# Norm panels made row block by row block, with sums and row inside the next panel, and rows of scales made from a repeated column and the identity

## The reference, cut to what matters

```python
def rmsnorm(x, g):
    return x * lax.rsqrt(jnp.mean(x * x, axis=-1, keepdims=True) + EPS) * g

# first block, after its two mixers (y_ssd, y_attn)
mixed = (g_ssd * y_ssd + (attention @ w_attn_out) * g_attn) @ w_o
x = x + rmsnorm(mixed, post_mix_norm)
h = rmsnorm(x, pre_mlp_norm)
x = x + rmsnorm(jnp.square(jax.nn.relu(h @ w_mlp_in)) @ w_mlp_out, post_mlp_norm)
# second block
h = rmsnorm(x, norm_mix_g)            # then w_in: gates, mLSTM, latent attention
q_a  = rmsnorm(c_q, cq_norm_g) @ w_uq # c_q, c_kv, k_r are columns of h @ w_in
kv   = rmsnorm(c_kv, ckv_norm_g) @ w_ukv
# q_nope, q_rope, k_nope per head and k_rope get a norm each, then rotation, attention
x = x + concat(y_m, y_a) @ w_out
h = rmsnorm(x, norm_x_g)              # cross attention over 256 memory rows;
q = rmsnorm(h @ wq_x); k = rmsnorm(mem_n @ wkv_x part)   # per head
x = x + cross_attention @ wo_x
h = rmsnorm(x, norm_ffn_g)
x = x + jnp.square(jax.nn.relu(h @ w_ff1)) @ w_ff2
```

## Time and profile before

| | us |
|---|---|
| median of 3 timed runs | 2132.68 (2130.52 to 2133.43) |
| the profiled execution's own time | 2122.09 |
| its span, first to last instruction | 2120.0 |
| PE busy | 1972.2 (93%), mean granted clock 0.965 of 2.4 GHz |
| POOL busy | 1546.5 (73%) |
| DVE busy | 917.0 (43%) |
| ACT busy | 654.6 (31%) |
| time of the chain that ended last, by engine | PE 77%, POOL 11%, DVE 7% |

### The profile page before, as it was taken

One profiled execution on the slowest core, in us unless ns is written; L12 is line 12 of the kernel. 1 busy time (PEld: TensorE's weight loads), 2 busy tenths in 40 slices (PEclk: granted clock), 3 DMA queues, 4 the chain that ended last, 5 costly groups with the idle time before them and its releaser, 6 DMA issues.

```text
span 2120.0 us, 26435 instructions
## 1 busy us (share of the span) xinstructions
PE 1972.2 (93%) x9749; PEld 1625.7 (77%) x9749; DVE 917.0 (43%) x1732; ACT 654.6 (31%) x1216; POOL 1546.5 (73%) x1379
## 2 busy tenths in 40 slices
PE   6999999999999999799999989888697889999998
PEld 4888888887878888578888867756366767888887
DVE  4566666641034434354014226754654055401421
ACT  4466666542045651131011002342231142200200
POOL 7799988797845449779889887542709808988985
PEclk9999999999999999899999999997898899999999
DMA  7222222123332223213333321111102302333232
GB/s 214 81 60 60 60 60 72 49 63 103 83 112 62 67 70 123 93 43 99 99 99 99 100 82 50 49 41 60 40 1 80 116 4 79 99 99 95 89 98 75
DMA packets 212121, 165.97 MB, mean 78 GB/s; under 512 B 13438, under 2 KB 208321, under 8 KB 211634
## 3 DMA queue, kind: packets, MB, share of 16 engines
q1 hardware_dynamic: 207126, 147.61, 23.6%
q10 hardware_dynamic: 4892, 17.01, 2.4%
HBM read 161.43 MB, written 7.37 MB: 80 GB/s over the span
## 4 chain that ended last, share of the span: by engine, by line
PE 77%; POOL 11%; DVE 7%; issue 2%; ACT 2%; DMA 0%; DVEq 0%; SPq 0%; ACTq 0%; POOLq 0%
PE bank L393 58%; POOL w_lo L2548 5%; PE bank L413 4%; POOL w_hi L2543 3%; PE bank L1338 3%; PE bank L1314 2%; PE bank L1324 1%; PE bank L2104 1%; POOL x_features L651 1%; POOL arena L1031 1%; PE bank L2113 1%; PE bank L1013 1%; DVE arena L1786 1%; PE bank L991 1%; PE bank L459 1%
## 5 line engine op out<-in xcount | busy, mean ns | idle before, releaser
L2543 POOL TENSOR_TENSOR w_hi<-w_raw,one 128x512 fp32r<-128x512 f32 (+2 forms) x520 | 529.7, 1050 | 500.5 <-PE bank L393 436.6
L2548 POOL TENSOR_TENSOR w_lo<-w_raw,w_hi 128x512 fp32r<-128x512 f32 (+2 forms) x600 | 745.7, 1274 | 34.6 <-ACT w_hi L1176 30.2
L393 PE MATMUL bank<-h_hi,w_hi 128*128 128x512 f32 (+1 forms) x1144 | 459.1, 401 | 39.3 <-DVE h_lo L622 16.7
L393 PE MATMUL bank<-h_hi,w_lo 128*128 128x512 f32 (+1 forms) x1144 | 444.6, 389 | 0.0
L393 PE MATMUL bank<-h_lo,w_hi 128*128 128x512 f32 (+1 forms) x1144 | 444.4, 388 | 0.0
L393 PE MATMUL bank<-a_hi,w_hi 128*128 128x512 f32 x896 | 351.5, 392 | 12.7 <-POOL w_lo L2548 8.2
L393 PE MATMUL bank<-a_lo,w_hi 128*128 128x512 f32 x896 | 350.2, 391 | 0.0
L393 PE MATMUL bank<-a_hi,w_lo 128*128 128x512 f32 x896 | 350.1, 391 | 0.0
L393 PEld LDWEIGHTS bank<-h_hi,w_hi 128*128 128x128 f32 x1144 | 219.2, 192 | 95.8 <-issue 18.8
L393 PEld LDWEIGHTS bank<-h_hi,w_lo 128*128 128x128 f32 x1144 | 219.0, 191 | 44.5
L393 PEld LDWEIGHTS bank<-h_lo,w_hi 128*128 128x128 f32 x1144 | 219.7, 192 | 38.4 <-issue 0.2
(11 more groups left out here) (380 smaller groups left out, 2728.7 us busy)
## 6 DMA issues: line engine op xcount, KB each, us to landing
w_raw<-in_w_in SPq DMA_DIRECT2D x32, 1024.0 KB, 5.3
w_raw<-in_w_ff SPq DMA_DIRECT2D x32, 1024.0 KB, 5.5
w_raw<-in_w_mlp_in SPq DMA_DIRECT2D x16, 1024.0 KB, 5.3
w_raw<-in_w_mlp_out SPq DMA_DIRECT2D x16, 1024.0 KB, 5.8
w_raw<-in_w_in SPq DMA_DIRECT2D x25, 512.0 KB, 4.4
w_raw<-in_w_ssd_out SPq DMA_DIRECT2D x8, 1024.0 KB, 5.8
bias_rows<-bias_row ACTq DMA_DIRECT2D x1, 4096.0 KB, 15.8
w_raw<-in_w_attn_out SPq DMA_DIRECT2D x4, 1024.0 KB, 5.3
```

The lines of the kernel that those rows point to most:

```text
L393: mm = pe.matmul(bank[:, 0:ntok], a, b[:, koff + k, 0:ntok], start=(k == 0 and n == 0), stop=(k == L.kb - 1 and n == 2))
L2543: pool.tensor_tensor(w_hi[:, slot, part], raw[:, slot, part], one[:].broadcast_to([P, n]), ALU.mult).then_inc(split_hi, 1)
L2548: ins = pool.tensor_tensor(w_lo[:, slot, part], raw[:, slot, part], w_hi[:, slot, part].bitcast(F32), ALU.subtract)
```

## The change

`pe_panel_rows` is a panel in which both output blocks advance together: at each k it waits once and then makes six products. It serves the first panel of `L_attn_out`, `L_o`, both feed-forwards, `L_if` and `L_qx`. `pe_panel_with_root` is a panel with the sum behind its first block and the row behind the fourth k step of its second; it replaces sum and row around panel 1 of both feed-forwards and panel 0 of `L_m[0]`. The diagonals are gone: a row is made of one product per token tile, whose stationary operand is the column of scales repeated 128 times (stride 0) and whose moving operand is the identity. TensorE waits for the reciprocal in their place.

```diff
+        def pe_panel_rows(pe, L, i, X, ready, koff=0):
+            xh, xl = X
+            slot = (L.p0 + i) % 2
+            blocks = [(L.b0 + i * L.nb + j, off) for j, off in enumerate(L.offs)]
+            pe.wait_ge(split_ready, L.p0 + i + 1)
+            for blk, _ in blocks:
+                pe.wait_ge(acc_free, blk - 3)
+            for k in range(L.kb):
+                pe.wait_ge(*ready(k))
+                for blk, off in blocks:
+                    c = k * L.w + off
+                    wh, wl = w_hi[:, slot, c:c + P], w_lo[:, slot, c:c + P]
+                    for n, (a, b) in enumerate(((wh, xh), (wh, xl), (wl, xh))):
+                        mm = pe.matmul(banks[blk % 4][:], a, b[:, koff + k, :], start=(k == 0 and n == 0), stop=(k == L.kb - 1 and n == 2))
+                    if k == L.kb - 1:
+                        mm.then_inc(acc_ready, 1)
+
+        def pe_panel_with_root(pe, L, i):
+            pe_panel(pe, L, i, i, h_x, only=0)
+            root_sum_pe(pe)
+            pe_panel(pe, L, i, i, h_x, only=1, ks=range(0, 4))
+            root_row_pe(pe)
+            pe_panel(pe, L, i, i, h_x, only=1, ks=range(4, DB))
...
         def root_row_pe(pe):
-            pe.wait_ge(nx_diag, nx_n["sum"])
-            pe.matmul(NROW[:], ones[:], NROOT, start=True, stop=True).then_inc(nx_row, 1)
+            pe.wait_ge(nx_inverse, nx_n["sum"])
+            for t in range(T):
+                mm = pe.matmul(NROW[:, t * P:(t + 1) * P], nstat[:, t:t + 1].broadcast_to([P, P]), ident[:], start=True, stop=True)
+            mm.then_inc(nx_row, 1)
...
-            dve_link(dve.reciprocal(nstat, nstat))
+            dve.reciprocal(nstat, nstat).then_inc(nx_inverse, 1)
             row_dve(dve)
...
         def row_dve(dve):
-            n = nx_n["acc"] // DB
-            dve.tensor_tensor(NROOT.rearrange("p (t f) -> p t f", t=T), ident[:].unsqueeze(1).broadcast_to([P, T, P]),
-                              nstat.unsqueeze(2).broadcast_to([P, T, P]), ALU.mult).then_inc(nx_diag, 1)
-            dve.wait_ge(nx_row, n)
+            dve.wait_ge(nx_row, nx_n["acc"] // DB)
...
-                    pe_panel(pe, L1, 0, 0, h_x, ready=normed(("pre_mlp", "ffn")[k]))
-                    root_sum_pe(pe)
-                    pe_panel(pe, L1, 1, 1, h_x)
-                    root_row_pe(pe)
+                    pe_panel_rows(pe, L1, 0, h_x, normed(("pre_mlp", "ffn")[k]))
+                    pe_panel_with_root(pe, L1, 1)
...
-            pe_linear(pe, L_if, h_x, ready=normed("mix2"))
-            root_sum_pe(pe)
-            pe_panel(pe, L_m[0], 0, 0, h_x)
-            root_row_pe(pe)
+            pe_panel_rows(pe, L_if, 0, h_x, normed("mix2"))
+            pe_panel_with_root(pe, L_m[0], 0)
             pe_panel(pe, L_m[0], 1, 1, h_x)
...
         def rows_pe(pe, n, tiles=T):
-            pe.wait_ge(la["diag"], n + 1)
+            pe.wait_ge(la["inverse"], 1 if n == 0 else 2 if n < 3 else 3 if n < LATENT_ITEMS else 4)
             if n >= 3:
                 pe.wait_ge(la["out"], n - 2)
-            pe.matmul(ROW_RING[n % 3][:, 0:tiles * P], ones[:], DIAG[n % 2][:, 0:tiles * P], start=True, stop=True).then_inc(la["row"], 1)
+            col = 4 * n if n < LATENT_ITEMS else CROSS_ITEMS[n - LATENT_ITEMS][0]
+            for t in range(tiles):
+                mm = pe.matmul(ROW_RING[n % 3][:, t * P:(t + 1) * P], lstat[:, col + t:col + t + 1].broadcast_to([P, P]), ident[:],
+                               start=True, stop=True)
+            mm.then_inc(la["row"], 1)
...
         def norms_dve(dve, first, last):
             outs = norm_outputs()
-            diag_dve(dve, first, 4 * first)
             for n in range(first, last):
-                if n + 1 < last:
-                    diag_dve(dve, n + 1, 4 * (n + 1))
                 scale_dve(dve, n, *outs[n])
```

More of the change, by code:

```diff
@@ L525, in build_program @@
         nx_sq, nx_acc, nx_sum, nx_root, nx_hi, nx_lo, nx_add = (sem(f"nx_{k}") for k in ("sq", "acc", "sum", "root", "hi", "lo", "add"))
-        NSQ, NACC, NROOT = [A(8192, 512), A(8704, 512)], A(9216, 512), A(9728, 512)
-        nx_diag, nx_row, nx_post = sem("nx_diag"), sem("nx_row"), sem("nx_post")
+        NSQ, NACC = [A(8192, 512), A(8704, 512)], A(9216, 512)
+        nx_inverse, nx_row, nx_post = sem("nx_diag"), sem("nx_row"), sem("nx_post")
         nstat, NROW = small[:, 104:104 + T], banks[5]
@@ L1605, in mix_pe @@
         def mix_pe(pe):
-            pe_linear(pe, L_attn_out, a_x, ready=counted(tp_free, tp_n["pe"] - DB))
+            for i in range(L_attn_out.n):
+                if i == 0:
+                    pe_panel_rows(pe, L_attn_out, i, a_x, counted(tp_free, tp_n["pe"] - DB))
+                else:
+                    pe_panel(pe, L_attn_out, i, i, a_x)
             for i in range(L_o.n):
-                pe_panel(pe, L_o, i, i, a_x, koff=8, ready=counted(mix_lo, 0))
+                if i == 0:
+                    pe_panel_rows(pe, L_o, i, a_x, counted(mix_lo, 0), koff=8)
+                else:
+                    pe_panel(pe, L_o, i, i, a_x, koff=8)
                 if i == 1:
@@ L2031, in build_program @@
         DIAG = [t[:, 15, :] for t in (a_free_hi, a_free_lo)]
-        la = {k: sem("la_" + k) for k in ("rope", "sw", "v", "vt", "vl", "ang", "sin", "sq", "ev", "sum", "root", "diag", "row", "out", "fin", "cos", "turned")}
+        la = {k: sem("la_" + k) for k in ("rope", "sw", "v", "vt", "vl", "ang", "sin", "sq", "ev", "sum", "root", "inverse", "row", "out", "fin", "cos", "turned")}
         RR = slice(64, 128)
@@ L2278, in latent_dve @@
             dve.wait_ge(la["root"], 1)
-            dve_link(dve.reciprocal(lstat[:, 0:4], lstat[:, 0:4]))
+            dve.reciprocal(lstat[:, 0:4], lstat[:, 0:4]).then_inc(la["inverse"], 1)
             norms_dve(dve, 0, 1)
@@ L2286, in latent_dve @@
             dve.wait_ge(la["root"], 2)
-            dve_link(dve.reciprocal(lstat[:, 4:12], lstat[:, 4:12]))
+            dve.reciprocal(lstat[:, 4:12], lstat[:, 4:12]).then_inc(la["inverse"], 1)
             norms_dve(dve, 1, 3)
@@ L2308, in latent_dve @@
             dve.wait_ge(la["root"], 3)
-            dve_link(dve.reciprocal(lstat[:, 12:60], lstat[:, 12:60]))
+            dve.reciprocal(lstat[:, 12:60], lstat[:, 12:60]).then_inc(la["inverse"], 1)
             norms_dve(dve, 3, 7)
@@ L2388, in cross_pe @@
                     root_row_pe(pe)
-            pe_linear(pe, L_qx, a_upper_x, ready=normed("norm_x"))
+            pe_panel_rows(pe, L_qx, 0, a_upper_x, normed("norm_x"))
+            pe_panel(pe, L_qx, 1, 1, a_upper_x)
             for h in range(X_HEADS):
@@ L2420, in cross_act @@
                 kvx_act(act, b)
-            act.wait_ge(nx_diag, nx_n["root"])
+            act.wait_ge(nx_inverse, nx_n["root"])
             for h in range(X_HEADS):
@@ L2444, in cross_dve @@
             dve.wait_ge(la["root"], 4)
-            dve_link(dve.reciprocal(lstat[:, 0:cross_cols], lstat[:, 0:cross_cols]))
+            dve.reciprocal(lstat[:, 0:cross_cols], lstat[:, 0:cross_cols]).then_inc(la["inverse"], 1)
             outs = [(XK[:, h, :], colv("xk")) for h in range(X_HEADS)] + [(XQ[:, h, :], colv("xq")) for h in range(X_HEADS)]
[L2447 to L2451, removed]
+            for i, out_ in enumerate(outs):
+                scale_dve(dve, LATENT_ITEMS + i, [out_], tiles=CROSS_ITEMS[i][1])
             dve.drain().then_inc(xa_q, 1)
```

## The result

The changed kernel took 2103.77 us (median of 4 runs, 2097.02 to 2111.39) against 2132.5 (2130.52 to 2133.43) of the kernel before on the same chip: ratio 0.9878, 95% interval 0.9849 to 0.9907. The forecast of 2098.1 was 5.7 us too low, inside its range. Timed again later, the same kernel took 2096.16 (five runs, 2090.68 to 2098.47) against 2127.51, ratio 0.9851 (0.9825 to 0.9878), and that profile has a span of 2094.4. Both are needed to read the result.

A forecast was written before the change was run, and what follows sets the result against it. TensorE carries 77% of the chain, so only its gaps and work put on it count. 4.0 + 5.2 + 1.4 + 10.5 + 10.5 + 3.0 = 34.6 us, from 2132.7 to 2098.1; bounds add up to 13.5 and 44 us saved.

The forecast's parts named there:

- First feed-forward: Panel by rows, with sum and row inside the next panel, at the first feed-forward: saves 4.0 us (2.2 to 6.0).
- the collision: POOL's weight split runs beside DVE's additions of squares, 1.40 us each against 0.78; TensorE waits before the sum.
- Second norm: Second block's norm: row at 1296.7 instead of 1301.95, so DVE's convolution chain starts earlier: 5.2 us (3.4 to 7.4).
- Second feed-forward: Second feed-forward: panel 0 gains nothing, the 1.5 us gap behind the row goes: 1.4 us (0.5 to 1.5).
- the 10.6: Saving at both feed-forwards and the second block's norm together, with the collision of squares and split: 10.6 us.
- Latent rows 1 and 2: Row products replace two diagonals: TensorE goes on 7.0 us earlier, and a higher clock behind gives 3.5: 10.5 us.
- Rival (c): At latent rows 1 and 2 POOL's long instruction still holds DVE: 8.4 us less saving, 2106.5; chance 0.09.
- Twelve rows: Twelve rows before attention: row products replace diagonals, POOL's rotation then releases attention: 10.5 us (4.8 to 11.1).
- Cross rows: Eight cross rows before the cross attention: row products replace diagonals, ending at 1703.2: 3.0 us (0.5 to 5).
- (a): Rival: the clock stays at 1.2 GHz in the row stages, saving 22.9 us, 2109.8; chance 0.18.
- (d): Rival: the repeated column's load isn't hidden under the product before it, so 21 us slower, 2154; chance 0.03.
- The six terms: First feed-forward 4.0, second norm 5.2, second feed-forward 1.4, latent rows 10.5, twelve rows 10.5, cross rows 3.0: 34.6 us.

The follow-up runs named there:

- Panels alone: The changed kernel with the diagonals of the latent and cross rows back; panels by rows, sum and row inside a panel stay: 2117.53 us, ratio 0.9947.
- the experiment: The changed kernel with DVE's diagonals and one product per row back for latent rows 1 and 2 alone: 2109.86 us, ratio 0.9907 to the kernel before.
- the idle products: The changed kernel with three unneeded 512-column float32 products on TensorE between the twelfth row and attention's first scores: 2084.61 us, ratio 0.9788 to the kernel before.
- before_again: The kernel before, unchanged, run and profiled once more: 2128.31 us, ratio 0.9997.

## Why the prediction was right, and where it was not

**First feed-forward, 4.0:** 5.2 and 5.0. Panel 0's end and the collision came as worked out, the wait before the sum was half as long; the additions took 1.35, and three rather than 1.7 escaped the split. (The prediction's 0.43 for a product at the low clock is not twice 0.227, which is 0.45; it moves panel 0's end by 0.1.) **Second norm, 5.2:** 6.4 and 4.2. Its mechanism held in one of the two: DVE was the last before the sum only in the execution near 2096, and that one lost 1.6 us to the clock behind it. **Second feed-forward, 1.4:** -0.1 and 1.5. Panels alone gave 10.0 for the 10.6.

**Latent rows 1 and 2, 7.0 + 3.5:** TensorE resumed 7.1 us earlier after the reciprocal, 7.2 by the experiment. The clock behind it gave 4.3 more in the execution near 2096, and in the other it took all back. Rival (c) is out.

**Twelve rows, 10.5:** 10.8 to 10.9, released by POOL. At 2.4 GHz the records of a row start 0.11 us apart and at 1.2 GHz 0.21 (0.12 and 0.215 forecast); the low level held for the first two rows and a bit, the forecast had three. **Cross rows, 3.0:** 3.2 and 4.2. Rivals (a) and (d) are out as the main course: the loads stay hidden, and the clock rises within the rows.

**The step that failed** is the end of the one on the twelve rows. I found that POOL's rotation would be late and shifted attention by 10.5, and did not ask what TensorE's new stand would do to the clock in the stage behind it, though I had priced the clock inside each row stage. Its price is 8.0 to 9.6 us in attention beside the first profile of the kernel before, and the idle products gave it back.

**That the total came so near is in part luck.** The forecast took its stages from one profile of the kernel before, one of its fastest executions, and subtracted them from a median 10.6 us higher. That profile has attention at 30.4 us, but `before_again`, close to the median, has 35.2: part of the price that the change pays there the kernel before often pays too. Between `before_again` and the execution near 2096 lie 31.9 us, much as between the medians (31.3). The six terms give 38.4 of them, more than the 34.6; attention takes back 4.8, the mLSTM 2.0. Terms that were too small and a stage put at nothing cancel. With the idle products the same change saved 2.1%, 45 us.

**Open:** why the same instructions with the same stands run at half the clock in one execution and not in another (latent products 38.0 or 49.8 us in the changed kernel; mLSTM 149.7 to 154.6 us in the kernel before, 153.1 and 155.8 in the changed one). The experiments show that stands of TensorE matter and that what is won in one stage can be lost in the next; they don't show what decides.

## What to carry to other kernels

When an edit makes another engine the last to arrive, price the stand of TensorE twice: once as time, and once as the clock of the stage behind it. Three us of products that nobody needs, put in the stand, are worth a trial; in the kernel before, whose stand was 0.89 us, they brought nothing. A panel made row by row needs the sum moved into the next panel, and each should be looked at with the other engine's queue beside it. And take the stages from more than one profile of the kernel before, or a fast execution of it will pass for its usual time.

## What the runs showed of the hardware beyond that

A column repeated by stride 0 as stationary operand costs nothing over a plain one: its loads took 0.19 us in the median (0.34 at most, 168 of them), as the plain ones of the earlier trace rows, and lay under the products. The kernel before itself varied from 2121 to 2140 us over all its executions, with mean granted clocks from 0.956 to 0.966, so one profile of each kernel can show a difference of 10 us where the medians differ by 29.
